# Gate projections by one Strassen step, and top-256 selection by counting against a threshold

## The reference, cut to what matters

```python
h = rms_norm(x, norm_g[l]) * (1.0 + scale[:, None]) + shift[:, None]
proj = h @ w_in[l]
(qa, ka, va, za, aa, ba, qb, ckv, zb, qi, ki, wi, gl) = jnp.split(proj, pts, axis=-1)
...
oa = rms_norm(oa, gdn_norm_g[l]).astype(x.dtype).reshape(B, T, GDN_W) * jax.nn.silu(za)
...
dots = jnp.einsum('bqhd,bsd->bqhs', qi.astype(f32), k_idx32)
score = jnp.einsum('bqh,bqhs->bqs', wi.astype(f32), jax.nn.relu(dots))
admissible = key_pos[None, :] <= t[:, None]
score = jnp.where(admissible[None], score, -jnp.inf)
_, sel = lax.top_k(score, k_sel)
...
ob = jnp.einsum('bthc,chd->bthd', o_lat, w_uv[l]).reshape(B, T, DSA_W) * jax.nn.silu(zb)
...
ga, gb = jnp.split(jax.nn.sigmoid(gl), 2, axis=-1)
out = (ga * ya + gb * yb) @ w_out[l]
```

## Time and profile before

| | us |
|---|---|
| median of three runs | 1510.22 (1508.64 to 1511.46) |
| the profiled execution's own span | 1508.5 |
| PE, DVE, ACT, POOL busy in it | 1469.4, 1052.1, 570.2, 408.7 |
| scores | 107 to 153 |
| gate projections on PE | 152.4 to 486.3 |
| selection and masks on DVE | 153.6 to 479.0 |
| first matmul of the next phase | 488.92 |

### The profile page before, as it was taken

How to read it: one execution, slowest core, us unless ns; L and a number is a source line. 1 busy time by engine, 2 the same in 40 slices (tenths; PEclk the granted TensorE clock), 3 DMA queues, 4 the chain that set the end, 5 groups by cost and what they waited for, 6 DMA issues and landing times.

```text
span 1508.5 us, 26403 instructions
## 1 busy us (share of the span) xinstructions
PE 1469.4 (97%) x9630; PEld 901.4 (60%) x9638; DVE 1052.1 (70%) x2032; ACT 570.2 (38%) x1223; POOL 408.7 (27%) x475
## 2 busy tenths in 40 slices
PE   7999999999999999999999999999999999999997
PEld 6455885444444466676676676655446787854444
DVE  3639999999997556778778776545724767748434
ACT  4528321111111435545555554333114666621111
POOL 0130114223331245324414313003002544456000
PEclk9999999999999999999999999999999999999999
DMA  9310223333313222222322212336663000055132
GB/s 373 100 54 5 74 77 102 111 106 105 102 66 115 75 56 71 82 63 57 86 56 59 86 48 75 110 89 220 200 226 116 30 16 30 15 208 190 49 112 84
DMA packets 133459, 146.94 MB, mean 97 GB/s; under 512 B 16898, under 2 KB 105578, under 8 KB 131692
## 3 DMA queue, kind: packets, MB, share of 16 engines
q1 hardware_dynamic: 120908, 124.24, 26.1%
q10 hardware_dynamic: 12320, 21.27, 3.9%
q0 software_dynamic: 128, 0.03, 0.0%
HBM read 114.40 MB, written 31.15 MB: 96 GB/s over the span
## 4 chain that ended last, share of the span: by engine, by line
PE 59%; DVE 3%; ACT 2%; POOL 2%; issue 1%; DMA 0%; SPq 0%; DVEq 0%; POOLq 0%
PE ps L92 15%; PE ps L94 15%; PE ps L93 14%; PE ps L1938 2%; PE ps L1418 1%; PE ps L1515 1%; PE ps L1470 1%; DVE g_o L1279 1%; PE ps L1476 1%; PE ps L1482 1%; PE ps L1456 1%; PE ps L1536 1%; PE ps L1464 1%; PE ps L1520 1%; PE ps L1519 1%
## 5 line engine op out<-in xcount | busy, mean ns | idle before, releaser
L92 PE MATMUL ps<-g_h_hi,g_piece_hi 128*128 128x512 f16 x544 | 207.3, 381 | 2.6 <-PEq L2130 2.6
L94 PE MATMUL ps<-g_h_hi,g_piece_lo 128*128 128x512 f16 x544 | 206.9, 380 | 0.0
L93 PE MATMUL ps<-g_h_lo,g_piece_hi 128*128 128x512 f16 x544 | 206.9, 380 | 0.0
L92 PE MATMUL ps<-g_h_hi,a_w_hi 128*128 128x512 f16 x448 | 169.9, 379 | 3.1 <-DVE g_h_lo L579 2.4
L94 PE MATMUL ps<-g_h_hi,a_w_lo 128*128 128x512 f16 x448 | 169.8, 379 | 0.0
L93 PE MATMUL ps<-g_h_lo,a_w_hi 128*128 128x512 f16 x448 | 169.8, 379 | 0.0
L668 DVE MATCH_REPLACE8 a_ada<-a_best,a_ada 128x1024 f32<-128x1024 f32 (+2 forms) x192 | 166.8, 877 | 0.0
L665 DVE MAX8 a_best<-a_ada 128x8 f32<-128x1024 f32 (+2 forms) x192 | 161.1, 881 | 0.7 <-DVE a_ada L654 0.3
L914 POOL TENSOR_TENSOR g_shared<-g_shared 128x120 f32<-128x120 f32 (+14 forms) x120 | 53.1, 442 | 203.0 <-DMA g_shared<-diagonal_blocks 192.7
L507 ACT ACTIVATE a_x<-ps 128x512 f32<-128x512 f32 x48 | 28.7, 597 | 196.5 <-PE ps L94 196.4
L92 PE MATMUL ps<-g_o,g_h_hi 128*128 128x128 f16 (+2 forms) x424 | 101.5, 266 | 1.0 <-DVE l_b L2059 1.0
(11 more groups left out here) (333 smaller groups left out, 3527.1 us busy)
## 6 DMA issues: line engine op xcount, KB each, us to landing
a_w<-in_w_in SPq DMA_DIRECT2D x17, 1024.0 KB, 5.6
g_piece<-in_w_in SPq DMA_DIRECT2D x34, 512.0 KB, 3.8
channel_gates<-a_x ACTq DMA_DIRECT2D x48, 256.0 KB, 2.0
g_shared<-diagonal_blocks SPq DMA_DIRECT2D x32, 256.0 KB
a_ada<-in_w_ada ACTq DMA_DIRECT2D x4, 1024.0 KB, 9.0
a_x<-in_x SPq DMA_DIRECT2D x8, 512.0 KB, 9.4
delta_gate<-a_x ACTq DMA_DIRECT2D x32, 128.0 KB, 1.8
g_shared<-sums_by_head SPq DMA_DIRECT2D x8, 512.0 KB, 4.1
```

The costliest lines, as they stand in the source:

```text
L92: pe.matmul(out, a_hi, b_hi, start=first, stop=False)
L93: pe.matmul(out, a_hi, b_lo, start=False, stop=False)
L94: return pe.matmul(out, a_lo, b_hi, start=False, stop=last)
```

## The change

**Projections.** A unit is now a 2 x 2 problem: its 256 columns in two halves of 128, the 1024 inner rows in two halves of 512, the tokens in two halves of 512. Winograd's form of Strassen's scheme makes the four result quarters from seven products of half size instead of eight. POOL makes four sums of weight quarters per unit (`weights`) and the low parts of all seven operands (`low`); ACT makes the high parts (`high`; for unit 0 POOL does). Four sums of token quarters are made once (`tokens` on DVE, `high_t` on ACT, `t_lo` on POOL), from a float32 copy of h that is now kept whole in `h32`, and the score stage waits for them (`t_low`). Several products accumulate in the same PSUM bank; in between ACT copies the bank's state out (`keep`), six times per unit, and PE waits for that (`kept`) before it goes on in the bank. POOL adds the held products to three of the four results (`joined`); the fourth, C21, is complete in the bank. ACT applies the gate's function in SBUF (`gate`), and SP now issues all stores (`result`), in line with its loads. z units use 128-wide matmuls, four token tiles per product, channel units 512-wide ones.

**Selection.** For the six tiles in two groups DVE counts how many scores reach a trial value (`count`, a tensor_scalar that also writes its sum), and sets or clears one bit of the trial value accordingly, from bit 30 to bit 0 (`compare`, `settle`; `decide` is one bit for both groups). Rows with fewer than 256 scores that are zero or more have their sign flipped first (`orient`). Where several scores equal the threshold, `finish` ranks them by position, with running sums over blocks of 16 and over the blocks, and writes the mask. The steps are written out in 16 turns of a Python loop; nothing makes DVE wait for the other engines there, but for the decay's step.

**Order at the end.** SP loads the second piece, waits for `masked`, writes the mask, loads the third piece, waits for the mask's DMA, and only then issues the four results of the last unit.

```diff
-            sp.dma_start(g.piece32[:], win[:, :, C_K:C_K + P]).then_inc(first_in, 16)
...
-            sp.wait_ge(first_ok, 1)
-            sp.dma_start(g.piece32[:], win[:, :, C_V:C_V + P]).then_inc(first_in, 16)
-            sp.wait_ge(first_ok, 2)
-            sp.dma_start(g.piece32[:], win[:, :, C_Q:C_Q + P]).then_inc(g.piece_in, 16)
-            sp.wait_ge(masked, NT)
-            sp.dma_start(g.mask_dram, mask).then_inc(mask_out, 16)
-            sp.wait_ge(mask_out, 16)
...
+                if u == UNITS - 1:
+                    sp.wait_ge(sum_rows_out, 32)
+                    sp.wait_ge(first_ok, 1)
+                    sp.dma_start(g.piece32[:], win[:, :, C_V:C_V + P]).then_inc(first_in, 16)
+                    sp.wait_ge(masked, NT)
+                    sp.dma_start(g.mask_dram, mask).then_inc(mask_out, 16)
+                    sp.wait_ge(first_ok, 2)
+                    sp.dma_start(g.piece32[:], win[:, :, C_Q:C_Q + P]).then_inc(g.piece_in, 16)
+                    sp.wait_ge(mask_out, 16)
+                result(u, C11)
+                result(u, C21)
+            result(UNITS - 1, C12)
+            result(UNITS - 1, C22)
+            for n in range(4):
+                sp.wait_ge(stored[n], 16 * UNITS // 2)
...
-            def split(s, arrived, free, n):
-                pool.wait_ge(w_in[s], arrived).then_inc(pool_alone, 1)
-                pool.wait_ge(proj, free).then_inc(pool_alone, 1)
-                nc.gpsimd.tensor_copy(w_hi[:, s], w32[:, s]).then_inc(w_cast, 1)
-                pool.wait_ge(w_cast, n + 1)
-                nc.gpsimd.tensor_tensor(w_lo[:, s], w32[:, s], w_hi[:, s], ALU.subtract).then_inc(w_ready, 1)
...
+            for n, block_of in enumerate((quarter(1, 1), quarter(1, 0), quarter(0, 0), quarter(0, 1))):
+                pool.wait_ge(t_cast, n + 1)
+                nc.gpsimd.tensor_tensor(t_lo[:, n], block_of, t_hi[:, n], ALU.subtract).then_inc(t_low, 1)
+
+            def low(v, x, of):
+                pool.wait_ge(own_cast if v == 0 else w_cast, x + 1 if v == 0 else 7 * (v - 1) + x + 1)
+                nc.gpsimd.tensor_tensor(op_lo[v % 2][:, x], of, op_hi[v % 2][:, x], ALU.subtract).then_inc(w_ready, 1)
+
+            def high(v, x, of):
+                if v == 0:
+                    nc.gpsimd.tensor_copy(op_hi[0][:, x], of).then_inc(own_cast, 1)
+
+            def joined(u, c, count, other, done):
+                pool.wait_ge(kept, 6 * u + count)
+                nc.gpsimd.tensor_tensor(slot_of(u, c), slot_of(u, c), other, ALU.add).then_inc(done, 1)
+
+            def weights(v):
+                a11, a12, a21, a22, total = part_of(v, 0, 0), part_of(v, 0, 1), part_of(v, 1, 0), part_of(v, 1, 1), pair_sum[v % 2]
+                pool.wait_ge(w_in[v % 2], 16 * (v // 2 + 1))
+                if v == 0:
+                    pool.wait_ge(q_mm, 8)
+                nc.gpsimd.tensor_tensor(total, a21, a22, ALU.add).then_inc(w_sum, 1)
+                pool.wait_ge(w_sum, 4 * v + 1)
+                nc.gpsimd.tensor_tensor(a21, a11, a21, ALU.subtract).then_inc(w_sum, 1)
+                high(v, A11, a11)
+                high(v, A12, a12)
+                high(v, A22, a22)
+                low(v, A11, a11)
+                pool.wait_ge(w_sum, 4 * v + 2)
+                pool.wait_ge(w_ready, 7 * v + A11 + 1)
+                nc.gpsimd.tensor_tensor(a11, total, a11, ALU.subtract).then_inc(w_sum, 1)
+                low(v, A12, a12)
+                pool.wait_ge(w_sum, 4 * v + 3)
+                pool.wait_ge(w_ready, 7 * v + A12 + 1)
+                nc.gpsimd.tensor_tensor(a12, a12, a11, ALU.subtract).then_inc(w_sum, 1)
+                high(v, S1, total)
+                high(v, S3, a21)
+                high(v, S2, a11)
+                if v == 0:
+                    pool.wait_ge(w_sum, 4)
+                high(v, S4, a12)
+                low(v, A22, a22)
+                if v:
+                    joined(v - 1, C11, 2, held[:, 0], first_sum)
+                low(v, S1, total)
+                low(v, S3, a21)
+                low(v, S2, a11)
+                low(v, S4, a12)
+
+            weights(0)
+            for u in range(UNITS):
+                if u + 1 < UNITS:
+                    weights(u + 1)
+                else:
+                    for n in range(2):
+                        pool.wait_ge(first_in, 16 * (n + 1))
+                        nc.gpsimd.tensor_copy(g.piece_hi[:, n], g.piece32[:]).then_inc(first_cast, 1)
+                        pool.wait_ge(first_cast, n + 1)
+                        nc.gpsimd.tensor_tensor(g.piece_lo[:, n], g.piece32[:], g.piece_hi[:, n], ALU.subtract).then_inc(first_ok, 1)
+                        if n == 0:
+                            joined(u, C11, 2, held[:, 0], first_sum)
+                joined(u, C22, 5, held[:, 1], third_sum)
+                joined(u, C12, 6, held[:, 2], second_sum)
...
+            def product(u, x, of, b, first):
+                w_h, w_l, (o_h, o_l) = op_hi[u % 2][:, x], op_lo[u % 2][:, x], of
+                if u < 4:
+                    for j in range(4):
+                        tok, out = slice(j * P, (j + 1) * P), g.ps[:, b * BANK + j * P:b * BANK + (j + 1) * P]
+                        for k in range(4):
+                            nc.tensor.matmul(out, o_h[:, k, tok], w_h[:, k], start=first and j == 0 and k == 0, stop=False, skip_group_check=True)
+                            nc.tensor.matmul(out, o_h[:, k, tok], w_l[:, k], start=False, stop=False, skip_group_check=True)
+                            last = nc.tensor.matmul(out, o_l[:, k, tok], w_h[:, k], start=False, stop=k == 3, skip_group_check=True)
+                else:
+                    for k in range(4):
+                        nc.tensor.matmul(bank(b), w_h[:, k], o_h[:, k], start=first and k == 0, stop=False, skip_group_check=True)
+                        nc.tensor.matmul(bank(b), w_h[:, k], o_l[:, k], start=False, stop=False, skip_group_check=True)
+                        last = nc.tensor.matmul(bank(b), w_l[:, k], o_h[:, k], start=False, stop=k == 3, skip_group_check=True)
+                last.then_inc(proj, 1)
...
+            pe.wait_ge(t_low, 4)
+            for u in range(UNITS):
+                x, y, z = (3 * (u % 2) + n for n in range(3))
...
+                pe.wait_ge(w_ready, 7 * (u + 1))
+                if u >= 2:
+                    pe.wait_ge(gated, gate_count(u - 2, C21))
+                product(u, A11, B11, x, True)
+                if u >= 2:
+                    pe.wait_ge(kept, 6 * (u - 1))
+                product(u, A12, B21, y, True)
+                pe.wait_ge(kept, 6 * u + 1)
+                product(u, S2, T2, x, False)
+                product(u, S1, T1, z, True)
+                pe.wait_ge(kept, 6 * u + 3)
+                product(u, S3, T3, x, False)
+                pe.wait_ge(kept, 6 * u + 4)
+                product(u, S4, B22, z, False)
+                pe.wait_ge(kept, 6 * u + 5)
+                product(u, A22, T4, x, False)
...
+            def high_t(n):
+                act.wait_ge(t_ok, n + 1)
+                nc.scalar.copy(t_hi[:, n], (quarter(1, 1), quarter(1, 0), quarter(0, 0), quarter(0, 1))[n]).then_inc(t_cast, 1)
...
+            def keep(u, count, to, bank_of, free=None):
+                act.wait_ge(proj, 7 * u + count)
+                if free is not None and u >= 2:
+                    act.wait_ge(stored[4 * (u % 2) + free], 16 * (u // 2))
+                nc.scalar.copy(to, bank(bank_of)).then_inc(kept, 1)
+
+            def gate(u, c, ready):
+                act.wait_ge(ready, u + 1)
+                nc.scalar.activation(slot_of(u, c), slot_of(u, c), ACT.Silu if u < UNITS // 2 else ACT.Sigmoid).then_inc(gated, 1)
+
+            for u in range(UNITS):
+                x, y, z, v = 3 * (u % 2), 3 * (u % 2) + 1, 3 * (u % 2) + 2, u + 1
+                a11, a12, a21, a22, total = part_of(v, 0, 0), part_of(v, 0, 1), part_of(v, 1, 0), part_of(v, 1, 1), pair_sum[v % 2]
+                if v < UNITS:
+                    act.wait_ge(w_in[v % 2], 16 * (v // 2 + 1))
+                    if u:
+                        act.wait_ge(proj, 7 * u)
+                high(v, A11, a11)
+                high(v, A12, a12)
+                high(v, A22, a22)
+                keep(u, 1, slot_of(u, C11), x, C11)
+                high(v, S1, total)
+                high(v, S3, a21)
+                if u == 0:
+                    act.wait_ge(acc, len(units))
+                else:
+                    act.wait_ge(first_sum, u)
...
+            def tokens(n, to, a, b, op):
+                dve.wait_ge(lo_ok if n == 0 else t_ok, 2 * KD if n == 0 else n)
+                nc.vector.tensor_tensor(to, a, b, op).then_inc(t_ok, 1)
+
+            b11, b12, b21, b22 = quarter(0, 0), quarter(1, 0), quarter(0, 1), quarter(1, 1)
             for n in range(8):
                 half, m = divmod(n, 4)
                 cols = slice(half * BANK, (half + 1) * BANK)
+                if n == 5:
```

(85 more changed lines are left out.)

334 lines of the change are left out of this document (191 added, 143 removed).

## The result

The changed kernel takes 1545.55 us (median; 1542.46 to 1546.78) against 1510.84 for the kernel before on the same chip: a ratio of 1.0233, 95% interval 1.0212 to 1.0255. The forecast was 1557, slower. The profiled execution has a span of 1543.5 us.

A forecast was written before the change was run, and what follows sets the result against it. PE was taken to bound the projections, with DVE's selection 7 us behind, and DVE the score stage. Next phase at 537, 48 later: 1508.5 + 48 + 1.7 = 1558, stated as 1557 us; range 1490 to 1590.

The forecast's parts named there:

- PE: Gate projections: seven products per unit instead of eight take 295 us together, 39 us less; 16 units at 19.0 us.
- POOL's price: Projections: POOL's sums and low parts take 15.5 to 18.0 us per unit, 17.6 with hand-overs.
- Score stage: Before the projections: DVE's score additions take turns with POOL's first-unit operands, +12 us; scores end at 165.
- The bit: DVE's counting, 31 bits: 5.8 us each bare, 9.9 us with waits for POOL.
- the walk through the slots: Counting: compare, power and xor wait for POOL instructions of 1.3 us each; 8 slots a bit, 9.9 us with POOL's idling.
- A: Main case, selection on DVE: compare, xor and also power wait for POOL, 9.9 us a bit; 1557 us, chance 0.45.
- B: Rival, counting on DVE: power is free of the shared port, 7.7 us a bit; 1541 us, chance 0.27.
- The finish: End of DVE's selection: about 17 contending steps per tile, 8 us bare, 29 us when POOL is always running.
- C: Rival, selection on DVE: the shared port hardly matters, DVE is through by 395; 1474 us, chance 0.15.
- D: Rival, counting on DVE: the counts wait for POOL as well, 15.6 us a bit; 1620 us, chance 0.05.
- H: Rival, DVE's waits: half of each is real, 6.8 us a bit, masks at 474; 1503 us, chance 0.08.
- The turning point: Counting: faster than before needs masks by about 480, so 8.1 us a bit, or 6.1 if half the tiles finish under contention.

The follow-up runs named there:

- pool_idle: The changed kernel with GpSimd's weight sums, low parts and result sums cut from 512 to 8 columns from the third unit on: 1486.15 us, ratio 0.9849.
- select_only: The projections of the kernel before, with the changed kernel's selection by counting: 1510.11 us, ratio 0.9994.
- small_in_psum: The changed kernel with three small tiles of a bit (wanted, few, power) placed in a PSUM bank: 1507.74 us, ratio 0.9979.
- one_group: The changed kernel with all six tiles in one group, so one compare, power and xor per bit instead of two: 1525.12 us, ratio 1.0087.
- strassen_only: The changed kernel's projections with the old selection (MAX8 and MATCH_REPLACE8): 1522.08 us, ratio 1.0075.

## Why the prediction was right, point by point

**PE**: 16 units in 461.7 - 164.2 + 0.4 = 297.9 us, 18.6 each, against 19.0. In pool_idle 18.4. Right, and its saving off the path, as forecast. POOL's price was added up wrongly at its upper end: seven at 1.158 and seven at 1.60 are 19.3 us, not 18.0. It did no harm, since an f32 sum took 1.27 and a low part 1.16 where nothing held them.

**Score stage**: scores end at 166.2 and PE starts at 164.2 (forecast 165 and 164 to 165), POOL's 23 us of the first unit's operands (103.4 to 126.7, forecast 18) among DVE's additions. Right in sum, and partly by luck: the waits of the long additions are 8.4 us, not 12, and the stage starts 4.3 us later (112.1 against 107.8), which the working had put at nothing. Of these, 2.8 are there when DVE's small steps begin (107.08 against 104.24), after the part with the new casts and token sums (that these are the cause isn't shown), and 1.5 are in the small steps.

**Setup**: counting starts at 182.3, forecast 182.

**The bit**: bare 5.9 us (forecast 5.8), counts of 1.27 us for 1024 columns that never wait. The Trainium skill, SBUF — State Buffer, Who interferes with whom, says so of an accumulating tensor_scalar, and the traces agree: 186 counts, the longest 1.279 us, as in pool_idle. Waits: 2.9 us a bit, where the walk through the slots gave 4.1. This is the term that was mis-sized, 31 x 1.1 = 34 us, some 8 of which the forecast itself had left out by counting its last two bits without POOL. The walk let POOL's instructions follow each other without a gap at nearly every step; POOL was busy 238 of 273 us, 87%, and 21 of the 62 xors took 0.16, that is, found a gap.

**Does power wait?** The point between A (1557) and B (1541). 52 of 62 took 0.25 us or more, up to 0.85, and 3.30 in select_only: a three-element tensor_scalar waits. A's reason held, though the time is nearer to B's: B had the right sum from a premise that the trace refutes. The Trainium skill, Vector Engine (DVE) Microarchitecture Reference, 5.1 Performance modes, had let an odd count run on two ports, and the rows agree with it.

**The finish**: 54.7 us against 49.4 for six tiles and the pivots, five of them at 7.9 each without POOL (forecast 8) and the first 14.9, partly beside POOL's last sums. Under load a tile took 18.7 to 26.0 in small_in_psum; forecast 29.

**The tail**: 8.4 us from the last mask to the next phase, forecast 8.

**The sum**: forecast 537 for the start of the next phase, measured 518.7: -24 from the bits, +5.3 from the finish, +0.4 from the tail. "Everything after the barrier unchanged" was off by 5.2 us in this profile (1024.8 against 1019.6). Of these, 3.8 lie in the stretch where GpSimd and DVE meet, and less than one in the slower clock of PE's first twelve matmuls (0.43 us apart instead of 0.21), eight of which ran so before. So the path was 18 us shorter than forecast and the time only 11: the difference is mostly this rest, and that is luck.

**The rivals**: C (the port hardly matters) is refuted by 41 of 62 xors; what it gave as the time without waits, 1474, stands beside pool_idle's 1486, which still has the 12 us of the score stage. D (counts wait) is refuted by their length. H, half of each wait: the share was in fact 2.9 of 4.1. The turning point named, 8.1 us a bit, fits: at 8.8 the kernel is slower. No run has a bit between 7.7 and 8.8; one_group's 7.7 wasn't enough, but its first tile was finished beside GpSimd and took 24.9 us.

## What to carry to other kernels

Work that is given to GpSimd because it is idle is charged to DVE wherever DVE has short dependent steps on SBUF: a step of three elements costs as much as what is left of GpSimd's instruction, and 186 of them cost 90 us of counting here. Before moving such work, count DVE's instructions with two inputs in SBUF or of the fast form, not its busy time; and take them off the list: put one operand of a two-input instruction into PSUM, and let a wide tensor_scalar write an accumulator that isn't needed, if its slower form is shorter than the wait. Look both ways: the wide steps of the finish held GpSimd, and it was PE that stood still.

## What the runs showed of the hardware that was not expected

- No instruction of DVE's counting with one input in PSUM and one in SBUF waited for GpSimd: 124 of three columns, none above 0.17 us. The scan of 1024 columns took 2.29 us with its second operand in PSUM against 3.24 with both in SBUF.
- The fast form can be the slow one: 128x1024 f32 to f16, tensor_scalar, 0.75 us alone and 1.63 beside GpSimd; with an accumulator 1.27 beside GpSimd.
- One scan instruction over 1024 columns takes 2.29 us; with one more step behind it, it takes the place of some sixteen.
- Two instructions that start within 0.03 us of each other can go in either order, and 2 to 5 us of the next phase go with the order: 3.01 and 1.91 us for DVE's and GpSimd's in the changed kernel, 1.28 and 3.02 in strassen_only, with starts 0.02 and 0.03 us apart.
